# Feed-forward first matrices: weights stationary, tokens streamed, product column-major

## The reference, cut to what matters

```python
def swiglu(h, w_in, w_out):
    g, u = jnp.split(h @ w_in, 2, axis=-1)
    return (jax.nn.silu(g) * u) @ w_out
# per layer i, after the token mixer
x = layer_norm(ALPHA * x + (1.0 + g1) * y, ln_g[i, 0], ln_b[i, 0])
h = x * (1.0 + sc2) + sh2
x = layer_norm(ALPHA * x + (1.0 + g2) * swiglu(h, ffn_w_in[i], ffn_w_out[i]), ln_g[i, 1], ln_b[i, 1])
```

## Time and profile before

| | |
|---|---|
| median of 3 runs | 2546.2 us |
| the runs | 2548.71, 2543.21, 2546.2 us |
| span of the profiled execution (its own time is not listed apart) | 2543.3 us |
| PE busy | 2422.3 us, 95% |
| DVE busy | 1801.5 us, 71% |
| ACT busy | 1033.8 us, 41% |
| share of the chain that ended last: PE | 85% |

### The profile page before, as it was taken

How to read it: one execution, slowest core, us unless ns; L and a number is a source line. 1 busy time by engine, 2 the same in 40 slices (tenths; PEclk the granted TensorE clock), 3 DMA queues, 4 the chain that set the end, 5 groups by cost and what they waited for, 6 DMA issues and landing times.

```text
span 2543.3 us, 32932 instructions
## 1 busy us (share of the span) xinstructions
PE 2422.3 (95%) x12569; PEld 1926.6 (76%) x12569; DVE 1801.5 (71%) x2796; ACT 1033.8 (41%) x1218; POOL 35.2 (1%) x67
## 2 busy tenths in 40 slices
PE   5898789999999999999999999989999999999998
PEld 2475357778888888888878887768788888888886
DVE  6556987877778776877779886887687754455457
ACT  1353023464443444344463434464644344433442
POOL 0000000000000000000000000000000000000000
PEclk9998889999999999999999999999999999999999
DMA  9956988877888888887857886717588766656664
GB/s 339 331 186 253 356 291 299 276 218 257 299 274 299 287 272 281 285 291 268 268 169 256 282 282 201 220 64 238 179 303 286 246 194 190 190 190 192 190 220 144
DMA packets 310172, 627.35 MB, mean 247 GB/s; under 512 B 30240, under 2 KB 30656, under 8 KB 309760
## 3 DMA queue, kind: packets, MB, share of 16 engines
q1 hardware_dynamic: 305728, 611.35, 71.6%
q0 software_dynamic: 4288, 13.90, 1.9%
HBM read 623.05 MB, written 2.10 MB: 246 GB/s over the span
## 4 chain that ended last, share of the span: by engine, by line
PE 85%; DMA 6%; DVE 5%; issue 2%; ACT 2%; SPq 1%; DVEq 0%; ACTq 0%
PE psB L1946 38%; PE psA L1946 38%; DMA col_raw<-in_ada_w 4%; PE psM L1660 1%; PE psT L1617 1%; PE psM L1647 1%; DVE w_lo L997 1%; DMA w_raw<-in_s_in_w 1%; DMA w_raw<-in_s_glu_w 1%; ACT w_hi L708 1%; PE psT L1806 1%; DVE ada_acc L1014 1%; PE psM L1632 0%; DMA w_raw<-in_dsa_out_w 0%; DVE soft L1494 0%
## 5 line engine op out<-in xcount | busy, mean ns | idle before, releaser
L997 DVE TENSOR_TENSOR w_lo<-w_raw,w_hi 128x1024 fp32r<-128x1024 f32 x740 | 903.3, 1224 | 596.4 <-ACT w_hi L708 592.0
L708 ACT ACTIVATE w_hi<-w_raw 128x1024 fp32r<-128x1024 f32 x740 | 783.2, 1060 | 1151.7 <-PE psB L1946 465.5
L1946 PE MATMUL psB<-w_hi,hT_hi 128*128 128x512 f32 x1152 | 456.2, 396 | 4.1 <-DVE w_lo L997 4.0
L1946 PE MATMUL psA<-w_hi,hT_hi 128*128 128x512 f32 x1136 | 448.0, 394 | 12.6 <-DVE w_lo L997 5.5
L1946 PE MATMUL psB<-w_hi,hT_lo 128*128 128x512 f32 x1152 | 448.9, 390 | 0.0
L1946 PE MATMUL psB<-w_lo,hT_hi 128*128 128x512 f32 x1152 | 448.6, 389 | 0.0
L1946 PE MATMUL psA<-w_hi,hT_lo 128*128 128x512 f32 x1136 | 443.2, 390 | 0.0
L1946 PE MATMUL psA<-w_lo,hT_hi 128*128 128x512 f32 x1136 | 442.9, 390 | 0.0
L1014 DVE SCALAR_TENSOR_TENSOR ada_acc<-ada_raw,csil,ada_acc 128x512 f32<-128x512 f32 x420 | 314.1, 748 | 14.1
L1946 PEld LDWEIGHTS psA<-w_hi,hT_hi 128*128 128x128 f32 x1136 | 213.5, 188 | 61.7 <-issue 13.5
L1946 PEld LDWEIGHTS psB<-w_hi,hT_hi 128*128 128x128 f32 x1152 | 216.4, 188 | 55.1 <-DVE w_lo L997 6.0
(11 more groups left out here) (357 smaller groups left out, 2120.0 us busy)
## 6 DMA issues: line engine op xcount, KB each, us to landing
w_raw<-in_ffn_w_in SPq DMA_DIRECT2D x352, 512.0 KB, 4.6
ada_raw<-in_ada_w SPq DMA_DIRECT2D x448, 256.0 KB, 5.1
w_raw<-in_ffn_w_out SPq DMA_DIRECT2D x176, 512.0 KB, 4.7
col_raw<-in_ada_w SPq DMA_DIRECT2D x160, 512.0 KB, 6.7
w_raw<-in_dsa_in_w SPq DMA_DIRECT2D x112, 512.0 KB, 4.7
w_raw<-in_s_glu_w SPq DMA_DIRECT2D x64, 512.0 KB, 5.5
w_raw<-in_s_in_w SPq DMA_DIRECT2D x32, 512.0 KB, 4.0
w_raw<-in_dsa_out_w SPq DMA_DIRECT2D x32, 512.0 KB, 5.3
```

Of the source, the lines that this page charges most:

```text
L708: nc.scalar.activation(high(u), w_raw[:, u % RING], ACT.Copy).then_inc(w_hi_ready, 1)
L997: V.tensor_tensor(low(u), w_raw[:, u % RING], high(u).bitcast(F32), ALU.subtract).then_inc(w_lo_ready, 1)
L1946: ins = MM(PS[s][:, t, 0:r.width], a_[:, kt, tok], b_[:, kk, 0:r.width], start=kt == 0 and m == 0, stop=k == r.units - 1 and kk == UK - 1 ...
```

## The change

In all feed-forward blocks but the first of each layer (10 of 11 blocks a layer, 20 in all) the operands of the first matrix change places. The 128 x 128 weight tile is loaded, and the 256 tokens stream through it. The product stands column-major in PSUM, which is the layout that the second matrix needs, so the 8 transposes of the block go. ACT now copies `stg[1]` itself into `aT_hi`, and DVE subtracts from `stg[1]`; both stay at the same place of their queues. The second matrix waits for a new semaphore, `a_lo_ready`. The first block of each layer keeps its old form, transposes included.

```diff
@@ counts of the runs
+            turned_blocks = r.n if r.kind != "ff" else int(r.before == "ln")
+            turn += r.turns * turned_blocks
+            aT_turned += turned_blocks if r.kind == "ff" else 0
+            aT_direct += r.n - turned_blocks if r.kind == "ff" else 0
+        def fixed(r, i):
+            return r.kind == "ff" and not (r.before == "ln" and i == 0)
+        def direct(r, i):
+            return r.direct0 + i + (r.before != "ln")
@@ ACT, turned
-                if r.kind == "ff" and s == 1:
+                if r.kind == "ff" and s == 1 and fixed(r, i):
+                    act.wait_ge(ps_free[1], r.use[1] + i + 1)
+                    nc.scalar.activation(aT_hi[:, 4 * i:4 * i + 4].rearrange("p a t -> p (a t)"),
+                                         stg[1][:].rearrange("p a t -> p (a t)"), ACT.Copy).then_inc(a_hi_ready, 1)
+                elif r.kind == "ff" and s == 1:
                     read_T(r, i, 0, aT_hi[:, 4 * i:4 * i + 4], hi=True)
@@ DVE, turned
+                if r.kind == "ff" and s == 1 and fixed(r, i):
+                    vec.wait_ge(a_hi_ready, direct(r, i))
+                    V.tensor_tensor(aT_lo[:, 4 * i:4 * i + 4].rearrange("p a t -> p (a t)"), stg[1][:].rearrange("p a t -> p (a t)"),
+                                    aT_hi[:, 4 * i:4 * i + 4].rearrange("p a t -> p (a t)").bitcast(F32), ALU.subtract
+                                    ).then_inc(a_lo_ready, 1)
@@ PE, turn
-                if r.kind == "ff" and s == 1:
+                if r.kind == "ff" and s == 1 and not fixed(r, i):
                     turn_T(r.turn + i + 1, [(ps_free[1], r.use[1] + i + 1)], lambda t, j: stg[1][:, t, j * P:(j + 1) * P])
@@ PE, operands
-                    pe.wait_ge(T_free, ff_turn + k // 2 + 1)
+                    if fixed(ff_run, k // 2):
+                        pe.wait_ge(a_lo_ready, direct(ff_run, k // 2))
+                    else:
+                        pe.wait_ge(T_free, ff_run.turn + 1)
@@ PE, new
+            def products_fixed(s, k, u, hi, lo):
+                for kk in range(UK):
+                    kt = k * UK + kk
+                    for j in range(NB // P):
+                        place = PS[s][:, j // 2, j % 2 * SEQ:(j % 2 + 1) * SEQ]
+                        for m, (a_, b_) in enumerate(((hi, high(u)), (hi, low(u)), (lo, high(u)))):
+                            ins = MM(place, b_[:, kk, j * P:(j + 1) * P], a_[:, kt], start=kt == 0 and m == 0 and j % 2 == 0,
+                                     stop=kt == KT - 1 and m == 2 and j % 2 == 1)
+                return ins
@@ PE, main loop
+                        elif fixed(r, i):
+                            ins = products_fixed(s, k, u + n, hi, lo)
```

More of the change, by code:

```diff
@@ L267, in build @@
         T_full, T_hi, T_free = sem("T_full"), sem("T_hi"), sem("T_free")
+        a_hi_ready, a_lo_ready = sem("a_hi_ready"), sem("a_lo_ready")
         rope_ready, rows_landed, row_used = sem("rope_ready"), [sem("rows_landed0"), sem("rows_landed1")], sem("row_used")
@@ L324, in build @@
         READ_AT, WEIGH_AT = 5, 7
-        unit = turn = hs = aT_parts = norms = 0
+        unit = turn = hs = aT_turned = aT_direct = norms = 0
         roped = 1
@@ L335, in build @@
                 norms += r.before == "ln"
-            r.unit, r.turn, r.use, r.roped, r.aT0 = unit, turn, list(use), roped, aT_parts
+            r.unit, r.turn, r.use, r.roped, r.aT0, r.direct0 = unit, turn, list(use), roped, aT_turned, aT_direct
             unit += r.per * r.n
             r.turns = {"u": 2, "rope": 2, "idx": 2, "ff": 1, "ki": 1}.get(r.kind, 0)
-            turn += r.turns * r.n
+            turned_blocks = r.n if r.kind != "ff" else int(r.before == "ln")
+            turn += r.turns * turned_blocks
             use[0] += r.n if r.kind != "ki" else 0
@@ L342, in build @@
             roped += r.n * r.blocks if r.kind in ("rope", "idx", "ki") else 0
-            aT_parts += r.n if r.kind == "ff" else 0
+            aT_turned += turned_blocks if r.kind == "ff" else 0
+            aT_direct += r.n - turned_blocks if r.kind == "ff" else 0
         runs[-1].final = True
@@ L2029, in _ @@
                 if r.kind == "ff":
-                    ff_turn = r.turn
+                    ff_run = r
 _INS = ["x", "c", "positions", "ada_w", "ada_b", "ln_g", "ln_b", "s5_in_w", "s5_a_re", "s5_a_im", "s5_log_dt", "s5_b_re",
```

## The result

The changed kernel takes 2579.7 us against 2545.2 us for the kernel before, measured beside it: 34.5 us more, a ratio of 1.0137 with a 95% interval of 1.0125 to 1.0149. The forecast was 2530 us with a range of 2524 to 2558. It was wrong, also in sign: the kernel became slower.

What follows compares the result with a forecast made beforehand. PE alone was taken to set the pace. 18 turns at 0.89 us gave -16.0 us, the copies and exchanged operands 0, so the 2546.2 us median becomes 2530 us; range 2524 to 2558.

Steps and rivals of the forecast that it cites:

- the price of the exchanged pair: First matrix of 20 feed-forward blocks: 7680 pairs of 128 loaded and 256 streamed columns start every 113.3 ns, cost 0.
- the turns: Transposes in the changed feed-forward blocks: 0.89 us of PE's time each, 18 of 20 gained, 16.0 us.
- the stream's cost goes strictly by columns and has no fixed part: Key projection's 256-column matmuls start 113 ns apart, half of 226.7 for 512, so halving the stream adds nothing.
- the third: Rival for the exchanged pairs: the load sets the pace; at 117 to 120 ns, 2558 to 2582 us, chance 0.14.
- the upper bound: Pair price of 120 ns, from key projection matmuls right after transposes; 51 us if all 7680 pairs ran so.
- The stream of L1737: Plain float32 matmuls of 128 columns, a full load each, 111 ns a pair; taken as most resembling the exchanged pair.
- pairs whose loads are not hidden at all: Rival for the exchanged pairs: 169 ns a short pair, 427 us more, 2957 us; chance 0.02.
- the third parts: Last turned block of each layer's third part: the 0.89 us becomes idle time before the fifth unit, nothing gained.
- ACT's longer copy: ACT's copy from `stg[1]` instead of PSUM: 1.06 us instead of 1.01, covered by ACT's free time, cost 0.
- Weight supply: Rival: layer 0 really waits for weights, so only layer 1's 9 turns count; 2538 us, chance 0.04.
- the DMA share: DMA engines in a layer 0 block: share goes from 0.90 to 0.92 as blocks shorten, still hidden.

Runs made afterwards that it cites:

- e4: Changed kernel with 272, 288 and 192 columns streamed in parts 0, 1 and 2 instead of 256, 128 loaded: 125.3, 131.7 and 111.7 ns a pair.
- e13: Changed kernel with other PSUM places: banks in turn (part 0), one place (part 1), only 240 tokens streamed (part 2): 120.0, 120.0 and 111.7 ns a pair.
- e1: Changed kernel with tokens loaded as before and 512 weight columns streamed, still no transposes: 2528.1 us against 2541.3 for the kernel before, ratio 0.9942.
- e7: Changed kernel with two matmuls for three, one of 512 and one of 256 columns: 346.7, 350.8 and 353.6 ns a couple by part; 2555.2 us.
- e8: Changed kernel with 320, 384 and 448 columns streamed in parts 0, 1 and 2, 128 loaded: 146.7, 173.3 and 202.7 (in places 206.7) ns a pair.
- e10: Kernel before with the stream shifted 16 columns (part 0) or 8 (part 1), or loaded tile shifted 16 (part 2): 230, 232.2 and 233.3 ns a pair.
- e12: Changed kernel with 80, 64 and 32 weight columns loaded in parts 0, 1 and 2: 113.3, 113.3 and 117.8 ns a pair (one half with 32: 113.3).
- e3: Changed kernel with 124, 120 and 96 weight columns loaded in parts 0, 1 and 2: mostly 117.3, 117.3 and 116.0 ns a pair.

## Why the prediction was wrong

**The step that failed** is the price of the exchanged pair: "I take 113.3, because the stream that most resembles it [...] ran at the speed of the slower half without a remainder. Cost 0." It took the slower of two paces, 113.3 ns for the stream and 111 for the loads, as the pace of both together. In the changed kernel every steady pair takes 120.0 ns. That is 6.67 ns over the slower half, 7680 times, and so the 51.2 us; with the 16.0 us of the turns it turns the sign.

Part of that step was "the stream's cost goes strictly by columns and has no fixed part". As a bound it stands: no steady stretch of 256 columns or more ran below 0.4427 ns a column, and a pair with 128 loaded columns right behind a long one runs at it within 1.5 ns, at eight lengths. As the price of a steady sequence it fails: with 128 loaded columns only the long pairs of 512 reach it, and 256 to 448 columns take 3 to 8 ns more. One may also write the steady pair as its columns at 2.4 GHz and 13.3 ns (exact at 256, 320, 384 and 512), and then the change pays for 3840 more pairs: 51.2 us again. The sum is the same; the first pairs of the blocks don't fit that form (86 ns at 192 columns, where it gives 93.3, and 113 at 256).

**The rival that was right in size** was the third, with a chance of 0.14 and 2558 to 2582 us at 117 to 120 ns. That 120, which I took as the upper bound, was the true value is partly luck: it was read off a few pairs of 80 loaded columns right after transposes, which settle at 113.3, while the pairs of the change stay at 120.0. Its mechanism, a load slower than the stream, does not hold in that form: a load of under 120 ns would be hidden behind 272 or 320 columns, and these pairs take 4.9 and 5.0 ns over their columns x 0.4427. That load and stream slow each other is not refuted.

**The stream of L1737**, by which I chose the lower end, showed the limit of loads, 111 ns, and nothing of the price of this pair: its matmuls are of another kind (plain float32, 128 columns). Runs e4 and e13 met a like limit, 111.7 ns, at 192 and 240 columns. From 240 to 256 columns the pace jumps from 111.7 to 120.0, so at 256 neither limit is the pace.

**The rules.** By the rule of the Trainium skill, "TensorE: Matmul & The Clock Gate", Part 3, The mechanism, a load overlaps matmuls only where row groups differ. The prediction put pairs whose loads are not hidden at all at 169 ns; at 120.0 it is not so here. What I left out was a rule with a fixed part. The Trainium skill, "TensorE: Matmul & The Clock Gate", Back-to-back issue gap, gives the gap of an isolated matmul as the columns over 2.4 GHz and a fixed 2.5 ns. The steady pairs here have nearly that form at 256 to 512 columns, but with 11.7 to 13.3 ns (more at 448) in place of 2.5. The form speaks against halving the stream. By the figure of that page of the Trainium skill, though, the 3840 added pairs would cost 9.6 us, an estimate from that 2.5 ns, which is less than the 16.0 us gained: it would not have turned the forecast.

**What was right.** The turn is worth 0.89 us, and 18 of 20 count (e1; its interval of 10 to 19 us holds the 16.0). In the third parts it became idle time in both layers. ACT's longer copy (1.04 us, not the 1.06 expected) and DVE's show no cost. 160 transposes are gone. Weight supply held, as PE had no idle time in changed blocks; the DMA share fell from 0.90 to 0.82 in a layer 0 block (654.60 to 701.53), since the blocks became longer.

**Open** is why short pairs in sequence take 120.0 ns. Shown: it depends on what runs ahead (113 ns behind a long pair), on the number of loaded columns, on the addresses of the loaded and of the streamed operand (not for shifts by 64 or 128 columns), and at some settings on the last interruption; it does not depend on the place in PSUM. That load and stream get in each other's way in reading SBUF would fit the addresses. It is only argued, and the small loads beside 512 columns, which cost more and not less, don't follow from it. A run in which two matmuls share one load would test whether the added loads or the added matmuls are what costs; there is none.

## What to carry to other kernels

A gain per block has to be held against what its pairs of load and matmul cost more: here a block saved 0.89 us of transposes and paid 6.7 ns on each of 384 pairs, 2.56 us. Two paces that were measured apart, and lie within 2 ns of each other, bound the pace of both together from below and do not give it; the row to look for is one with both sizes at once. Read a pace over several blocks, as the same code had two paces in e7, e8, e10, e12 and e3. Where the sum turns its sign within 2 ns, or 2%, of an unmeasured price, the forecast is no better than an even guess between the price's bounds.

## What was not expected of the hardware

A steady float32r pair with 128 columns loaded took 120.0 ns at 256 columns and 226.7 at 512, and 111.7 at both 192 and 240 (e4, e13). The first such pair behind one of 512 columns took 86 ns at 192 columns, 113 at 256 and 199 at 448, within 1 ns of 0.4427 ns a column. Shifting either operand by 4 to 32 columns changed a pair by -2 to +7 ns: it made short pairs faster (118.0 against 120.0 ns) and long pairs slower (up to 233.3 against 226.7 ns). Loading 32 columns instead of 128 made the long pair slower, 231.7 ns. An interruption of about 1 us could leave the same code at another pace for whole halves: 354 or 346.7 ns a couple in e7, 202.7 or 206.7 ns a pair in e8.
